# Moving the first activation buffer of a two-layer fp32 stack by 32 bytes in each SBUF partition

## Chip, core and metric

The kernel runs on one core of a Trainium2 chip. The metric is the device time of one execution in microseconds. The three runs shown for the kernel before lie between 2882.34 and 2883.41 us, with a median of 2883.28 us.

## What is computed

Two transformer-like layers on one sequence of 256 tokens with 2048 channels, all in fp32. The first layer has an input projection into a state-space mixer and an RWKV mixer, an output projection, cross attention to 256 memory tokens, and a feed-forward block of width 8192. The second has an input projection, windowed attention beside an S5 state-space branch, gated branch projections, and a gated feed-forward block of width 5632. Cut to its dense products:

```
u = rms_norm(x) @ w_in;  x = x + concat(ssd(u), rwkv(u)) @ w_out
x = x + cross_attention(rms_norm(x), rms_norm(mem), wq, wk, wv, wo)
x = x + square(relu(rms_norm(x) @ ffn_w1)) @ ffn_w2;  x = rms_norm(x)
proj = rms_norm(x) @ w_in_2;  attn, y = window_attention(proj), s5(proj)
x = x + (sig(ga)*(attn @ w_branch_attn) + sig(gs)*(glu(y) @ w_branch_ssm)) @ w_out_2
h = rms_norm(x);  x = x + (h@up_val * gelu(conv(h@up_gate))) @ w_down;  out = rms_norm(x)
```

## The kernel before

**Layout.** Channels lie on the 128 partitions, tokens along the free dimension. `x` is [128, 16, 256]. An operand of a dense product is kept as two parts whose sum is the fp32 value, a high part and a low part, both of type fp32r. An activation buffer holds both parts of each tile of 128 channels side by side: `[P, KT, 2, T]`, so one part of one tile is 256 values, 1024 bytes, in each partition.

**The stream of weights.** All dense products are phases of one pipeline (class `Stream`). A phase is a number of units (256 output columns of the weight), a unit is `nc` chunks (512 rows by 256 columns, 512 KB). For each chunk SP loads it into one of four ring slots (`raw`, line 320), ScalarE copies it to `hi` (`act_chunk`, line 379), VectorE writes `lo = raw - hi` (`split_low`, line 473), and TensorE multiplies it (`unit`). A chunk is 24 matmuls: two output halves by four channel tiles by a trio of part products. The trio is, with the stationary operand first and the moving operand second,

```
eng.matmul(out, self.hi[:, slot, cols], a[:, 0, :], start=opens, stop=False)
eng.matmul(out, self.hi[:, slot, cols], a[:, 1, :], start=False, stop=False)
ins = eng.matmul(out, self.lo[:, slot, cols], a[:, 0, :], start=False, stop=closes)
```

(lines 670, 671, 672). One phase, `wv` (kind "tok"), has the roles the other way round (lines 665 to 667): the activations `a[:, 0 or 1, toks]` are stationary and the 256 weight columns of `hi`, `hi`, `lo` are moving. After a unit VectorE reads its sums out of PSUM (`evacuate`), and ScalarE, VectorE or GpSimd write the next activations.

**Which activation buffer each phase reads.** There are 928 chunks. The first activation buffer `a0` is the moving operand of 568: `w_in` (14 + 6 + 4 units of 4), the two halves of `w_out` (16 each), `wk` (32), four quarters of `ffn1` (32 each), `w_in_2` (7 + 6 + 10 units of 4), `glu` (2 + 2), `br_ssm` (8), `up_gate` and `up_val` (22 units of 4 each). It is the stationary operand of the 32 chunks of `wv`. The other 328 read `a1` (`wq`, `wo`, four quarters of `ffn2`), `a2` (`w_out_2`, `down`) or `ah` (`br_attn`). Matmuls outside the pipeline are fp32 and belong to the mixers, the attentions and the norms.

**Places in a partition.** Tensors are laid on a stack one behind the other, and `room` tensors push the next one to a chosen address modulo `LINE` = 512 bytes. With the sizes in the code the places are these, in bytes modulo 512, before the change:

| tensor | place | tensor | place |
|---|---|---|---|
| x | 128 | a0 | 160 |
| consts, prm, rstd, root, sq, eps | 160 | sq2, gains | 192 |
| raw (all rings) | 160 | hi (all rings) | 224 |
| lo (all rings) | 352 | a1, a2, ah | 160 |
| ua, ub, u, kx, qx, vx, s_tab | 160 | s_xr | 192 |
| tb | 224 | th | 288 |

All rows of `a0`, `hi` and `lo` that one matmul reads begin at the place of their tensor, because 256 columns are 1024 bytes and half a unit is 512.

Of the kernel before, what the change touches and what calls it, by code (L numbers as in the profile page):

```python
# [25 lines left out]
P = 128  # L26
T = 256
D = 2048
KT = D // P
# [3 lines left out]
BASE = 128 + SCRATCH  # L33
LINE = 512
ACT_AT = 160
PART_AT = ACT_AT + 64
CK = 4
RING = 4
# [55 lines left out]
class Params:  # L94


    def __init__(self):
        self.at, self.n = {}, 0
# [6 lines left out]
PARAMS = Params()  # L105
# [85 lines left out]
class Stream:  # L191


    def __init__(self, nc, stack, dram):
        self.nc, self.dram = nc, dram

        def sb(name, shape, dt=F32):
            return stack.enter_context(nc.sbuf_tensor(name, shape, dt))

        def sem(name):  # L200
            return stack.enter_context(nc.semaphore(name))

        self.x = sb("x", [P, KT, T])
        at = BASE + KT * T * 4
        room = sb("a0_room", [P, (ACT_AT - at) % LINE // 4])
        self.a0 = sb("a0", [P, KT, 2, T], F32R)
        self.consts = sb("consts", [P, dram["consts"].shape[1]])
        self.prm = sb("prm", [P, PARAMS.n])
        self.rstd = sb("rstd", [P, T])
        self.root = sb("root", [P, T])  # L210
        self.sq = sb("sq", [P, 2, T])
        self.eps = sb("eps", [P, 8])
        self.sq2 = sb("sq2", [P, 2, T])
        self.gg = sb("gains", [P, KT])
        at += (ACT_AT - at) % LINE + KT * T * 8 + 4 * dram["consts"].shape[1] + -(-PARAMS.n // 8) * 32 + 6 * T * 4 + 32 + KT * 4
        room = sb("stage_room", [P, (ACT_AT - at) % LINE // 4])
        self.acc = stack.enter_context(nc.psum_tensor("acc", [P, 4, 512], F32))
        self.work = stack.enter_context(nc.psum_tensor("work", [P, 4, 512], F32))

        self.s_raw = [sem(f"raw_loaded{i}") for i in range(RING)]  # L220
        self.s_hi = sem("high_split")
        self.s_lo = sem("low_split")
        self.s_used = sem("chunk_multiplied")
        self.s_free = sem("banks_read")
        self.s_link = sem("vector_link")
        self.s_evac = sem("evacuated")
        self.s_fin = sem("finished")
        self.s_pool = sem("low_written")
        self.s_sum = sem("squares_summed")
        self.s_root = sem("root_ready")  # L230
        self.s_rstd = sem("rstd_ready")
        self.s_ehigh = sem("emitted_high")
        self.s_elow = sem("emitted_low")
        self.s_ghigh = sem("gained_high")
        self.s_glow = sem("gained_low")
        self.s_esq = sem("emitted_squares")
        self.s_first = sem("first_norm_steps")
        self.s_mean = sem("second_mean")
        self.s_root2 = sem("second_root")
        self.total = dict(c=0, u=0, links=0, evac=0, fin=0, pool=0, gain=0, norm=0, emits=0)  # L240
# [15 lines left out]
    def ring(self, stack, tag, parts=True, raw=None):  # L256
# [3 lines left out]
        def sb(name, shape, dt=F32):  # L260
            return stack.enter_context(nc.sbuf_tensor(name + tag, shape, dt))
        place = sb("raw", [P, RING, CK * UNIT])
        self.raw = place if raw is None else raw
        room = sb("ring_room", [P, (PART_AT - ACT_AT) // 4])
        self.hi = sb("hi", [P, RING, CK * UNIT], F32R)
# [2640 lines left out]
```

## Time and profile before

| | us |
|---|---|
| median of three runs | 2883.28 |
| lowest and highest run | 2882.34, 2883.41 |
| span of the profiled execution | 2882.9 |
| PE busy | 2802.8 (97%) |
| DVE busy | 1823.4 (63%) |
| ACT busy | 1245.7 (43%) |
| POOL busy | 396.0 (14%) |
| DMA, share of 16 engines | 54.9% |

Matmuls are pipelined: the duration of one runs from its start until its results are out, and the next starts before that. So the sum over the instructions of a line can be more than the time they fill, and the rate of the engine is read from starts, or from how many instructions fill a stretch. The profiled execution has no time of its own beside its span here; the span is 0.4 us under the median run.

### The profile page before, as it was taken

What the parts mean: (1) busy time and instruction counts of PE and PEld (TensorE: products, weight loads), DVE (VectorE), ACT (ScalarE), POOL (GpSimd) and SP (SyncE); (2) the same over time, 40 slices, a digit from 0 to 9 for tenths busy, and PEclk for the clock granted to TensorE, in tenths of its full rate; (3) what the DMA queues carried; (4) which work ended last, traced back from release to release, by engine and by line L of the source; (5) the groups of instructions that cost most, each with busy time, mean ns of one, the idle gap of its engine ahead of it and who ended that gap; (6) DMA issues with size and microseconds to landing.
All of it is one profiled execution on the core that took longest, in us unless ns stands there. A gap on an engine that the chain in (4) does not pass through costs nothing.

```text
span 2882.9 us, 61146 instructions
## 1 busy us (share of the span) xinstructions
PE 2802.8 (97%) x24650; PEld 2752.2 (95%) x24650; DVE 1823.4 (63%) x2175; ACT 1245.7 (43%) x1511; POOL 396.0 (14%) x549
## 2 busy tenths in 40 slices
PE   8999699999999999999999999999999999999998
PEld 8999687999989999999999999998999999999998
DVE  6678747775435655655555668697667655665664
ACT  5355223544334543444434545434454443443444
POOL 0000230110002139300461210000110000010011
PEclk9999899999999999999999999999999999999999
DMA  6654002566635566666667565554555665556564
GB/s 235 195 192 147 16 31 88 191 189 204 190 102 164 190 197 190 219 213 189 197 194 236 191 195 163 193 196 157 193 192 189 197 192 193 193 188 199 184 198 149
DMA packets 138418, 514.10 MB, mean 178 GB/s; under 512 B 15360, under 2 KB 15616, under 8 KB 136960
## 3 DMA queue, kind: packets, MB, share of 16 engines
q1 hardware_dynamic: 138240, 511.58, 54.9%
q8 instruction: 129, 2.11, 0.3%
q14 instruction: 49, 0.40, 0.0%
HBM read 503.12 MB, written 8.40 MB: 177 GB/s over the span
## 4 chain that ended last, share of the span: by engine, by line
PE 64%; DVE 4%; issue 1%; ACT 1%; DVEq 0%; ACTq 0%
PE acc L670 21%; PE acc L671 21%; PE acc L672 21%; DVE lo L473 1%; PE work L2170 0%; ACT hi L379 0%; DVE s_xr L2514 0%; PE acc L2203 0%; DVE tb L543 0%; DVE sq L2523 0%; DVE ua L2514 0%; DVE ub L2514 0%; DVE s_xr L2505 0%; DVE sq L2503 0%; DVE ta L2522 0%
## 5 line engine op out<-in xcount | busy, mean ns | idle before, releaser
L670 PE MATMUL acc<-a,hi 128*128 128x256 f32 x5504 | 1527.0, 277 | 16.3 <-DVE lo L473 14.5
L671 PE MATMUL acc<-a,hi 128*128 128x256 f32 x5504 | 1521.5, 276 | 0.0
L672 PE MATMUL acc<-a,lo 128*128 128x256 f32 x5504 | 1521.4, 276 | 0.0
L473 DVE TENSOR_TENSOR lo<-qx,hi 128x1024 fp32r<-128x1024 f32 x704 | 896.4, 1290 | 674.6 <-ACT hi L379 672.9
L670 PEld LDWEIGHTS acc<-a,hi 128*128 128x128 f32 x5504 | 1035.3, 188 | 20.5 <-issue 14.8
L671 PEld LDWEIGHTS acc<-a,hi 128*128 128x128 f32 x5504 | 1035.3, 188 | 0.8 <-issue 0.5
L672 PEld LDWEIGHTS acc<-a,lo 128*128 128x128 f32 x5504 | 1035.3, 188 | 0.0
L379 ACT ACTIVATE hi<-qx 128x1024 fp32r<-128x1024 f32 x704 | 733.9, 1057 | 646.4 <-PE acc L672 629.0
L620 POOL TENSOR_TENSOR a<-th,a 128x512 f32 (+1 forms) x64 | 84.9, 1327 | 1381.2 <-ACT a L424 1381.1
L473 DVE TENSOR_TENSOR lo_x<-next_raw,hi_x 128x1024 fp32r<-128x1024 f32 x128 | 162.2, 1281 | 115.0 <-ACT hi_x L379 115.0
L670 PE MATMUL acc<-a,hi_in 128*128 128x256 f32 x768 | 215.4, 280 | 9.8 <-DVE lo_in L473 9.8
L670 PE MATMUL acc<-a,hi_x 128*128 128x256 f32 x768 | 215.8, 281 | 5.8 <-DVE lo_x L473 5.8
L672 PE MATMUL acc<-a,lo_in 128*128 128x256 f32 x768 | 213.8, 278 | 0.0
L671 PE MATMUL acc<-a,hi_in 128*128 128x256 f32 x768 | 213.8, 278 | 0.0
L671 PE MATMUL acc<-a,hi_x 128*128 128x256 f32 x768 | 212.8, 277 | 0.0
L672 PE MATMUL acc<-a,lo_x 128*128 128x256 f32 x768 | 212.8, 277 | 0.0
L379 ACT ACTIVATE hi_x<-next_raw 128x1024 fp32r<-128x1024 f32 x128 | 133.9, 1058 | 144.2 <-PE acc L672 94.9
L473 DVE TENSOR_TENSOR lo_in<-raw_in,hi_in 128x1024 fp32r<-128x1024 f32 x96 | 115.4, 1222 | 68.2 <-ACT hi_in L379 68.1
L670 PEld LDWEIGHTS acc<-a,hi_in 128*128 128x128 f32 x768 | 146.1, 190 | 11.2 <-DVE lo_in L473 9.7
L670 PEld LDWEIGHTS acc<-a,hi_x 128*128 128x128 f32 x768 | 144.9, 189 | 8.5 <-issue 5.8
L671 PEld LDWEIGHTS acc<-a,hi_in 128*128 128x128 f32 x768 | 146.0, 190 | 0.3 <-issue 0.2
L672 PEld LDWEIGHTS acc<-a,lo_in 128*128 128x128 f32 x768 | 145.9, 190 | 0.0
(503 smaller groups left out, 2779.2 us busy)
## 6 DMA issues: line engine op xcount, KB each, us to landing
qx<-in_ffn SPq DMA_DIRECT2D x256, 512.0 KB, 4.2
raw_in<-in_w_in SPq DMA_DIRECT2D x96, 512.0 KB, 4.3
qx<-in_w_in SPq DMA_DIRECT2D x92, 512.0 KB, 3.7
qx<-in_up_gate SPq DMA_DIRECT2D x88, 512.0 KB, 4.2
qx<-in_up_val SPq DMA_DIRECT2D x88, 512.0 KB, 4.3
qx<-in_down SPq DMA_DIRECT2D x88, 512.0 KB, 4.2
next_raw<-in_wq SPq DMA_DIRECT2D x32, 512.0 KB, 4.3
next_raw<-in_wk SPq DMA_DIRECT2D x32, 512.0 KB, 4.3
```

Of the source, the lines that this page charges most:

```text
L379: eng.activation(self.hi[:, slot, :], self.raw[:, slot, :], ACT.Copy).then_inc(self.s_hi, 1)
L473: eng.tensor_tensor(self.lo[:, slot, :], self.raw[:, slot, :], self.hi[:, slot, :].bitcast(F32), ALU.subtract).then_inc(self.s_lo, 1)
L620: eng.tensor_tensor(out[:, :, 1, :], self.th[:, s], out[:, :, 0, :].bitcast(F32), ALU.subtract).then_inc(self.s_pool, 1)
L670: eng.matmul(out, self.hi[:, slot, cols], a[:, 0, :], start=opens, stop=False)
L671: eng.matmul(out, self.hi[:, slot, cols], a[:, 1, :], start=False, stop=False)
L672: ins = eng.matmul(out, self.lo[:, slot, cols], a[:, 0, :], start=False, stop=closes)
```

## The change

A constant `A0_AT` = 192 takes the place of `ACT_AT` = 160 where the room ahead of `a0` is sized. `a0` and the eight tensors behind it, up to `gains`, lie 32 bytes further on; `stage_room` shrinks from 416 to 384 bytes, so that `u` and everything behind it stays at its address. `x` stays. No instruction is added, removed or moved on any engine: the programs are the same but for addresses.

```
+A0_AT = 192
...
-        room = sb("a0_room", [P, (ACT_AT - at) % LINE // 4])
+        room = sb("a0_room", [P, (A0_AT - at) % LINE // 4])
         self.a0 = sb("a0", [P, KT, 2, T], F32R)
...
-        at += (ACT_AT - at) % LINE + KT * T * 8 + 4 * dram["consts"].shape[1] + -(-PARAMS.n // 8) * 32 + 6 * T * 4 + 32 + KT * 4
+        at += (A0_AT - at) % LINE + KT * T * 8 + 4 * dram["consts"].shape[1] + -(-PARAMS.n // 8) * 32 + 6 * T * 4 + 32 + KT * 4
         room = sb("stage_room", [P, (ACT_AT - at) % LINE // 4])
```

| modulo 512 | a0 | hi - a0 | lo - a0 | a1, a2, ah |
|---|---|---|---|---|
| before | 160 | 64 | 192 | 160 |
| after | 192 | 32 | 160 | 160 |

## Rows read from the trace of the kernel before

**Rows 1.** The page: span, and each engine's busy time.
```profile
span 2882.9 us, 61146 instructions
PE 2802.8 (97%) x24650; PEld 2752.2 (95%) x24650; DVE 1823.4 (63%) x2175; ACT 1245.7 (43%) x1511; POOL 396.0 (14%) x549
```

**Rows 2.** Groups by line, shapes apart, PE: count, busy us, mean ns, idle before.
```profile
L670 PE MATMUL acc<-a,hi 128*128 128x256 f32 x5504 | 1527.0, 277 | 16.3 <-DVE lo L473 14.5 <-issue 1.8
L670 PE MATMUL acc<-a,hi_x 128*128 128x256 f32 x768 | 215.8, 281 | 5.8 <-DVE lo_x L473 5.8
L670 PE MATMUL acc<-a,hi_in 128*128 128x256 f32 x768 | 215.4, 280 | 9.8 <-DVE lo_in L473 9.8
L670 PE MATMUL acc<-ah,hi 128*128 128x256 f32 x128 | 35.6, 278 | 0.9 <-DVE lo L473 0.9
```

**Rows 3.** Busy time in stretches, PE: from:to, length, busy (matmuls), clock, DMA share, GB/s.
```profile
747.24:837.68 90.44, 90.44 (x770) 1.00 0.50 152
1143.25:1230.29 87.04, 87.04 (x770) 1.00 0.66 218
1230.29:1317.33 87.04, 87.04 (x770) 1.00 0.66 204
2585.60:2672.64 87.04, 87.04 (x770) 1.00 0.63 197
```

**Rows 4.** Groups by line of the stretch 747.24:837.68, phase `wv`.
```profile
L665 PE MATMUL acc<-hi_x,a 128*128 128x256 f32 x256 | 72.2, 282 | 0.0
L666 PE MATMUL acc<-hi_x,a 128*128 128x256 f32 x256 | 71.9, 281 | 0.0
L667 PE MATMUL acc<-lo_x,a 128*128 128x256 f32 x255 | 71.1, 279 | 0.0
```

**Rows 5.** Groups by line of the stretch 1143.25:1230.29, `ffn1` reading a0.
```profile
L670 PE MATMUL acc<-a,hi 128*128 128x256 f32 x257 | 70.9, 276 | 0.0
L672 PE MATMUL acc<-a,lo 128*128 128x256 f32 x256 | 70.7, 276 | 0.0
L473 DVE TENSOR_TENSOR lo<-qx,hi 128x1024 fp32r<-128x1024 f32 x32 | 43.3, 1367 | 36.7 <-ACT hi L379 36.7
L379 ACT ACTIVATE hi<-qx 128x1024 fp32r<-128x1024 f32 x32 | 33.8, 1060 | 31.5 <-PE acc L672 28.0 <-DMA qx<-in_ffn 3.2
```

**Rows 6.** Stretches with all engines: busy (x) of PE, PEld, DVE, ACT, POOL.
```profile
450.00:572.00 122.00, 116.24 (x926) 104.88 (x925) 87.73 (x126) 56.32 (x78) 13.57 (x11) 0.98 0.47 156
1743.00:1976.00 233.00, 225.89 (x1841) 215.70 (x1840) 203.98 (x315) 103.30 (x181) 0.00 (x0) 1.00 0.54 179
```

**Rows 7.** Groups by line, fp32 matmuls of 256 columns, PE.
```profile
L1731 PE MATMUL acc<-kx,qx 128*128 128x256 f32 x32 | 7.1, 379 | 0.0
L2438 PE MATMUL acc<-s_xr,s_tab 128*128 128x256 f32 x32 | 9.5, 379 | 0.0
L2438 PE MATMUL acc<-ua,s_tab 128*128 128x256 f32 x16 | 4.8, 379 | 0.0
L772 PE MATMUL acc<-f,consts 128*16 128x256 f32 x16 | 3.6, 380 | 0.0
```

**Rows 8.** Line 1731: duration min/median/max, first and last start.
```profile
L1731 PE MATMUL acc<-kx,qx x32: 379/379/379, 846.0 to 852.7; 128*128 128x256 f32 x32
```

**Rows 9.** Starts on PE and PEld (weight loads) in two short stretches, us.
```profile
1199.83 0.28 PE L670 MATMUL acc<-a,hi 128*128 128x256 f32 x1
1199.83 0.19 PEld L671 LDWEIGHTS acc<-a,hi 128*128 128x128 f32 x1
1199.94 0.28 PE L671 MATMUL acc<-a,hi 128*128 128x256 f32 x1
1199.95 0.19 PEld L672 LDWEIGHTS acc<-a,lo 128*128 128x128 f32 x1
```

**Rows 10.** Groups by line, VectorE, tensors at different places.
```profile
L543 DVE TENSOR_TENSOR tb<-acc,rstd 128x512 f32<-128x512 f32 x93 | 63.6, 684 | 0.4 <-PE acc L672 0.3
L496 DVE TENSOR_TENSOR x<-acc,x 128x512 f32 (+1 forms) x88 | 60.1, 683 | 13.3 <-PE acc L672 13.3
```

## The prediction

> **What bounds the kernel now.** I read the page first: PE is busy 97% of a span of 2882.9 us, DVE 63%, ACT 43% [rows 1]. So the end is set by the matmuls, and the change can only matter through what it does to their rate, or through another engine becoming so slow that it takes over. Next the groups by line, with shapes apart, to see whether the matmuls wait: of the three large groups of line 670 the idle time ahead is 16.3, 5.8 and 9.8 us, nearly all for VectorE's low part, in more than 7,000 matmuls [rows 2]. PE simply runs one matmul after the other.
>
> The durations in these groups are not the rate, since matmuls overlap. For the rate I took stretches that hold exactly one phase, which is 32 chunks or 768 matmuls (the view counts 770, because it also counts those that reach in over the edges). A phase of `ffn1` that reads a0 takes 87.04 us, the phase behind it that reads a1 takes 87.04 us, and one of `down` that reads a2 takes 87.04 us [rows 3]. That is 87.04 / 768 = 113.3 ns for each matmul of 256 columns, whichever buffer is moving, all of them at place 160. The exactness is what to see here: no phase is held up by data. The starts say the same, 1199.83 and 1199.94, and the load of the next weights starts within 0.01 us of the matmul beside which it runs, 1199.83 and 1199.95 [rows 9]. So PE reads two operands from SBUF at the same time nearly all the time: the moving one of this matmul and the stationary one of the next.
>
> One phase is different. `wv`, with the same 768 matmuls of the same shape, takes 90.44 us at the same full clock [rows 3], 117.8 ns each: 3.40 us more for the phase, 4.43 ns more for each. Its matmuls last 282, 281 and 279 ns [rows 4] against 276 and 276 [rows 5], with no idle time ahead of them in either. Nothing was late there. What differs is which operand is read from where: in `wv` the weight parts at 224 and 352 are moving and a0 at 160 is being loaded, so that the loaded operand lies 64 or 192 bytes behind the moving one, modulo 512; in the other phases it lies 64 or 192 ahead. I take this as the one sign in the trace that the pair of addresses, or the roles, can cost PE time without any wait on a semaphore.
>
> **The change, part by part.** It adds, removes and moves no instruction. It changes addresses of three kinds.
>
> First, a0 as moving operand. This is 568 of 928 chunks, 568 x 24 = 13,632 of 22,272 matmuls (the total is three times the 7,168 of line 670 and the 256 of line 665, [rows 2, 4]). The load of `hi` now lies 32 bytes ahead of the moving operand in place of 64, that of `lo` 160 in place of 192. No row shows such a pair, so the price is bounded from both sides. The one end is nothing: 113.3 ns holds at two distances, +64 and +192, and +160 lies between them. The other end is that each pays what `wv` pays, 4.43 ns: 13,632 x 4.43 = 60.4 us. I choose between them like this. The distance +160 is bracketed by two distances at which nothing is paid, so I take zero for the third of the matmuls beside which `lo` is loaded. The distance +32 is not bracketed: on its other side, past zero, the trace has only -64 and -192, and both pay. So I take the price for the two thirds beside which `hi` is loaded, 9,088 matmuls. In `wv` the two matmuls that move `hi`, at distance -64, have 6 and 5 ns of the 14 that the trio is longer (6 + 5 + 3), so they pay 11/14 of 3 x 4.43 = 13.3 ns, 5.2 ns each. 9,088 x 5.2 = 47.3 us.
>
> Second, what of this lies under other waits. In the phases that run beside the mixers and the window attention PE is not quite full: 116.24 of 122.00 us and 225.89 of 233.00 us [rows 6]. The a0 chunks in and next to such stretches are 16 + 16 (`w_out`), 24 + 40 (`w_in_2`, its last 16 units) and 12 (`glu`, `br_ssm`), 108 of the 568; their share of the sum is 108 x 16 x 5.2 ns = 9.0 us. PE's idle time there is 5.8 + 7.1 = 12.9 us, so it could take up all of it or none. Part of that idle time is a wait for things that themselves come after matmuls. I take half, 4.5 us off.
>
> Everywhere else a slower PE is fully on the path. In the stretch of `ffn1` VectorE's low parts take 43.3 us and then wait 36.7 us for ScalarE, whose copies take 33.8 us and wait 28.0 us for PE to free a slot [rows 5]: both are ahead and will only wait longer. That is also the cover for the third kind.
>
> Third, the engines' own accesses to a0, `consts`, `prm`, `rstd` and the others, now 32 bytes further. VectorE's reads of 128x512 take 684 ns with `rstd` (160) and `tb` (224), 683 ns with `x` (128) [rows 10], so place does not show, and I cost it at nothing. If the a0 writes did become slower, the cover is the 36.7 us of waiting in 87.04; the first units of a phase that waits for its activations are the only places without it. The fp32 matmuls with `consts` have the same answer: those of 256 columns last 379 or 380 ns with the moving operand at 160 (`kx`, `ua`), 192 (`s_xr`) or 224 (`f2`, shown as `f`) [rows 7]. Bound on the other side: 2,378 of the 24,650 matmuls stand outside the pipeline [rows 1]; if all of them read a moved tensor, which they do not, 1 ns each would be 2.4 us.
>
> a0 as stationary operand is `wv` alone, 768 matmuls; its distances go from -64 and -192 to -32 and -160. It could lose its 3.4 us or pay as much again. I take zero, and 3.4 us either way goes into the range.
>
> **Sum.** 47.3 - 4.5 = 42.8 us on the profiled execution's 2882.9 us gives 2925.7 us; the median run is 0.4 us above that span, so I forecast 2926 us.
>
> [...]
>
> **The rivals.**
>
> *No change (2883 us, 2877.5 to 2889).* The cost in `wv` comes from the roles: a stationary operand that is a piece of an activation tile, and a moving one that is a weight. Or place counts only in steps coarser than 32 bytes, such as 64 or 128. For it: a0, a1, a2 and ah, at four different absolute addresses, give 113.3 ns to the last digit [rows 3]. Against it: nothing, but those four have the same place modulo 512, so they are no test. The sum is 2883.3 plus nothing.
>
> *All pay (2944 us, up to 2948).* +160 pays too: 60.4 us, and `wv` 3.4 us more at worst. Against it stand the free distances on both sides of +160.
>
> [...]
>
> [...]
>
> **How the numbers follow.** Faster 0.13. No change 0.27. Slower 0.60: 0.37 for the forecast (2905 to 2935), 0.15 for all pay (2935 to 2948), 0.08 for a small price (2889 to 2905), such as one matmul of the trio alone or 1 to 2 ns each. Within 0.2%, 5.8 us, is about what a measurement of this kernel can tell from no change. The predicted time is the likeliest case's, 2926. The range runs from the low end of no change, 2877, to all pay with `wv` on top, 2948: it leaves out the faster case and the little that lies above, 0.03 or so, which is under 2 in 10. Slower holds most of the chance; its own range is 2889 to 2948.
>
> **What the profile after would show.** A phase of `ffn1` or `up_val` that reads a0 should take 87.04 + 768 x 2/3 x 5.2 ns = 89.7 us, and the phases that read a1 and a2 still 87.04. Within a trio the matmuls beside which `hi` is loaded should start 5 ns later and the one beside which `lo` is loaded not; all three later means all pay. [...] If the a1 and a2 phases change as well, the cause isn't the pair of addresses. DVE and ACT groups should keep their mean times, with longer waits for PE.

## The result

The changed kernel takes 2944.32 us (median of four runs, 2940.81 to 2947.74) against 2883.35 us before: 61.0 us more, a ratio of 1.021 with a 95% interval of 1.0196 to 1.0225. The forecast was 2926 us, with a range up to 2948: the result lies inside the range, above the band of 2905 to 2935 that I had given to the forecast itself and in the band of the rival "all pay".

The page of the changed kernel, its span and busy times, which answer to [rows 1]:

```profile
span 2939.0 us, 61146 instructions
PE 2863.7 (97%) x24650; PEld 2813.4 (96%) x24650; DVE 1824.2 (62%) x2175; ACT 1246.2 (42%) x1511; POOL 396.0 (13%) x549
```

PE is 60.9 us longer busy with the same 24,650 matmuls. DVE, ACT and POOL do the same work in the same time to within 0.8 us. So all of it is in the rate of the matmuls. (The span grew by 56.1 us only, since PE's idle time shrank by 4.8.)

The same phases as in [rows 3], PE alone: from:to, length, busy (matmuls), clock, DMA share, GB/s. In this order `wv`, `ffn1` on a0, `ffn2` on a1, `down` on a2:

```profile
761.67:852.13 90.46, 90.46 (x770) 1.00 0.49 151
1161.25:1252.13 90.88, 90.88 (x770) 1.00 0.66 211
1252.13:1339.18 87.05, 87.05 (x770) 1.00 0.64 203
2635.89:2722.94 87.05, 87.05 (x770) 1.00 0.64 196
```

The phase on a0 went from 87.04 to 90.88 us: 3.84 us for 768 matmuls, 118.3 ns each in place of 113.3, 5.0 ns more. The phases on a1 and a2 kept their 87.0 us, `wv` its 90.4. Line numbers in this kernel are one higher. In groups by line of the same `ffn1` stretch the trio stands like this, to be read against [rows 5]:

```profile
L672 PE MATMUL acc<-a,hi 128*128 128x256 f32 x257 | 72.1, 281 | 0.0
L671 PE MATMUL acc<-a,hi 128*128 128x256 f32 x257 | 72.1, 281 | 0.0
L673 PE MATMUL acc<-a,lo 128*128 128x256 f32 x256 | 71.9, 281 | 0.0
L474 DVE TENSOR_TENSOR lo<-qx,hi 128x1024 fp32r<-128x1024 f32 x33 | 43.4, 1328 | 40.4 <-ACT hi L380 40.3
L380 ACT ACTIVATE hi<-qx 128x1024 fp32r<-128x1024 f32 x32 | 33.8, 1058 | 34.3 <-PE acc L673 31.6 <-DMA qx<-in_ffn 2.7
```

All three are longer, 281 against 276 ns, not two of three. From start to start it is 118.0 ns behind line 671, 119.0 behind 672 and 118.0 behind 673, where the load of `lo` runs beside line 672. VectorE and ScalarE only wait longer, 40.4 and 34.3 us where it was 36.7 and 31.5.

The timeline of PE where `ffn1` on a0 begins (start, duration):

```profile
1161.38 0.28 PE L671 MATMUL acc<-a,hi 128*128 128x256 f32 x1
1161.50 0.28 PE L672 MATMUL acc<-a,hi 128*128 128x256 f32 x1
1161.62 0.29 PE L673 MATMUL acc<-a,lo 128*128 128x256 f32 x1
1161.74 0.28 PE L671 MATMUL acc<-a,hi 128*128 128x256 f32 x1
1161.86 0.28 PE L672 MATMUL acc<-a,hi 128*128 128x256 f32 x1
```

The starts are 0.12 apart where they were 0.11. In whole ns they are no longer alike: the steps repeat every twelve matmuls as 114, 119, 117, 123, 115, 116, 120, 124, 116, 115, 118, 123, on average 118.3.

Where the time came from, by the first matmul of each stage in the two traces:

| stage | later by, us | 5.0 ns times its a0 matmuls |
|---|---|---|
| w_in, up to the RWKV scan | 8.0 | 11.5 |
| both halves of w_out | 2.6 | 3.8 |
| wq, wk | 3.8 | 3.8 |
| wv, cross attention | -0.2 | 0 |
| wo, four times ffn1 and ffn2 | 15.4 | 15.4 |
| w_in_2, first 52 chunks to the state space | 6.1 | 6.2 |
| w_in_2, last 40 chunks | 0.3 | 4.8 |
| glu, br_attn, br_ssm | 0.5 | 1.4 |
| w_out_2 | -1.6 | 0 |
| gate, val, down, three times | 21.2 | 21.1 |
| sum (13,632 matmuls) | 56.1 | 68.2 |

In `w_out_2`, which reads a2, the trace before has a spell at the lower clock (granted 0.98 over the stage, 88.78 us) and the one after has none (1.00, 87.17 us). The same holds for one chunk of `w_in`, before and after:

```profile
262.67:267.14 4.47, 4.47 (x25) 0.62 0.80 257
271.83:274.77 2.94, 2.94 (x25) 1.00 0.88 304
```

Some 1.6 us of the 3.5 us that are missing in the first row of the table are this spell and no wait. The profiled execution after is the fastest of the four, 3.5 us under their median, which is the larger part of why 56.1 us stand under the 61.0 of the medians.

### The profile page after: what moved, and what is told of

Same layout as the page of the kernel before. It is cut to its first block, busy times and chain, and to the rows that moved or that the text cites. A ratio compares the mean times of both kernels' runs of the same rounds, so it can differ in the third digit from the quotient of the medians.

```text
span 2939.0 us, 61146 instructions
## 1 busy us (share of the span) xinstructions
PE 2863.7 (97%) x24650; PEld 2813.4 (96%) x24650; DVE 1824.2 (62%) x2175; ACT 1246.2 (42%) x1511; POOL 396.0 (13%) x549
## 4 chain that ended last, share of the span: by engine, by line
PE 65%; DVE 3%; issue 1%; ACT 0%; DVEq 0%; ACTq 0%
PE acc L673 21%; PE acc L671 21%; PE acc L672 21%; DVE lo L474 1%; PE work L2171 0%; ACT hi L380 0%; DVE s_xr L2515 0%; PE acc L2204 0%; PE work L2427 0%; DVE ua L2515 0%; DVE tb L544 0%; DVE x L1916 0%; DVE sq L2504 0%; PE work L2191 0%; DVE sq L2524 0%
## 5 line engine op out<-in xcount | busy, mean ns | idle before, releaser
L671 PEld LDWEIGHTS acc<-a,hi_x 128*128 128x128 f32 x768 | 145.4, 189 | 8.2 <-issue 5.6
L672 PEld LDWEIGHTS acc<-a,hi_x 128*128 128x128 f32 x768 | 145.3, 189 | 0.6 <-issue 0.5
```

## The experiments

Two theories at the start. A: what counts is the distance from the operand that is moving to the operand that is being loaded. B: what counts is the place of the moving operand, a multiple of 64 bytes (192) or not (160).

**e1: weight parts 32 bytes nearer, all activations at 160.**

```
-PART_AT = ACT_AT + 64
+PART_AT = ACT_AT + 32
...
-        room = sb("end_room", [P, (LINE - 128) // 4])
+        room = sb("end_room", [P, (LINE - 96) // 4])
```

> All activation buffers at 160 as before, the weight parts 32 bytes nearer: hi at 192, lo at 320, so that every phase has the distances that the change gave to a0 (32 and 160). Theory A, the distance from the moving operand to the loaded one sets the price: all 21,504 matmuls with activations moving pay 5.0 ns, about +107 us, 2990 us. Theory B, the place of the moving operand on a 64-byte border sets it: none of the phases pays, 2883 us, each phase of 32 chunks 87.0 us; only wv, whose moving operands then lie on such a border, may change, by about 4 us.

2985.51 us (two runs), ratio 1.0351, interval 1.0305 to 1.0397. Now the phases on a0 and on a1 both pay (PE in stretches):

```profile
1173.88:1264.76 90.88, 90.88 (x770) 1.00 0.65 209
1264.76:1355.64 90.88, 90.88 (x770) 1.00 0.63 196
```

The same 90.88 us as in the changed kernel, with no activation buffer moved. Theory B falls. The two runs lie 9.9 us apart, so the total is known less well than the phases.

**e2: everything 32 bytes on.**

```
-ACT_AT = 160
+ACT_AT = 192
```

> Everything is moved by 32 bytes together: activation buffers at 192, hi at 256, lo at 384, distances 64 and 192 as before. Theory A (distance): 2883 us, phases of 32 chunks at 87.0 us. Theory B (moving operand on a 64-byte border): every phase pays 5.0 ns per matmul, 21,504 x 5.0 = 107 us, about 2990 us, phases at 90.8 us.

2883.79 us (eight runs), ratio 0.9997, interval 0.9985 to 1.0008.

```profile
1143.15:1230.19 87.04, 87.04 (x770) 1.00 0.67 218
1230.19:1317.23 87.04, 87.04 (x770) 1.00 0.67 205
```

With a0 at 192 and the weight parts moved with it, the cost is gone to the last digit. Theory A holds so far: what counts is where the two operands lie to each other.

**e3: a0 at 224.** The changed kernel with `A0_AT = 224`, distances 0 and 128.

> a0 alone at 224, another 32 bytes on: distance to hi 0 and to lo 128, off the 64-byte border again. Theory A: at least the price of distance 32, so 2944 us or more. Theory B: back to 113.3 ns per matmul, 2883 us.

2950.57 us (two runs), ratio 1.0229, interval 1.02 to 1.0259. The a0 phase takes 91.47 us, 119.1 ns each, although 224 is no more a multiple of 64 bytes than the 160 at which it took 87.04 us.

**e6 and e7: one distance wrong at a time.** Both start from e2. In e6 `low_room` has 96 bytes in place of 128 (and `end_room` 32 more), which gives distances 64 and 160. In e7 `PART_AT` is `ACT_AT + 32` and `low_room` 160 bytes: 32 and 192.

> Activations at 192, hi at 256, lo at 352: distances 64 and 160. My forecast had zero for a lo at distance 160: then every phase stays at 87.0 us per 32 chunks, 2883 us. If lo at 160 pays by itself (a third of the price measured, about 1.7 ns per matmul on average), 88.3 us per phase and about 2920 us. If the trio pays whole as soon as one distance is off, 90.8 us per phase and about 2985 us.

> Activations at 192, hi at 224, lo at 384: distances 32 and 192. My forecast had 5.2 ns for two of three matmuls: 89.7 us per phase of 32 chunks, about 2955 us. If the trio pays whole as soon as one distance is off: 90.8 us per phase and about 2985 us. If only lo at 160 was what cost in the changed kernel: 87.0 us and 2883 us.

2966.39 and 2976.64 us (one run each). PE in the a0 phase, e6 first, then e7:

```profile
1167.11:1257.56 90.45, 90.45 (x770) 1.00 0.67 210
```
```profile
1175.68:1266.13 90.45, 90.45 (x770) 1.00 0.68 210
```

Either error alone costs 3.41 us of the 3.84 that both cost together, so the two prices do not add up. Within the trio the two kernels differ. In e6 the steps behind lines 670, 671 and 672 are 114.0, 123.3 and 116.0 ns, and the long one is the one beside which `lo`, the part that stands wrong, is loaded (starts on PE and on PEld):

```profile
1199.86 0.28 PE L671 MATMUL acc<-a,hi 128*128 128x256 f32 x1
1199.87 0.19 PEld L672 LDWEIGHTS acc<-a,lo 128*128 128x128 f32 x1
1199.99 0.28 PE L672 MATMUL acc<-a,lo 128*128 128x256 f32 x1
1200.10 0.28 PE L670 MATMUL acc<-a,hi 128*128 128x256 f32 x1
```

In e7 they are 118.7, 118.3 and 116.3 ns: the matmul beside which `lo` is loaded pays 5.0 ns although `lo` stands right. So a load that stands wrong costs at its own place and can cost beside a right one too; a sum of prices, one for each load, gives neither kernel. (The two totals differ by 10 us with equal long phases. 8.6 of them are there before `ffn1` begins, where e7 has 14 us more at the lower clock (mean granted clock over the whole span 0.989, in e6 0.992) and stretches of chunks at 120.0 ns.)

**e4: a table of single pairs.** 16 moving by 16 stationary places, each pair 36 matmuls long, one behind the other.

> A kernel that leaves out the whole computation but for a copy of x, and runs 36 back-to-back fp32r matmuls of 256 columns for each of 16 moving places by 16 stationary places (steps of 32 bytes modulo 512), with nothing on the other engines. Moving 160 with stationary 224 or 352 should take 113.3 ns each, moving 192 with 224 or 352 118.3 ns, moving 224 with stationary 160 118 ns. Theory A: the time is a function of the difference of the two places. Theory B: 113.3 for moving places at 32 modulo 64, 118 for multiples of 64, whatever the stationary place; then moving 224 or 352 with stationary 160 would be 113.3 here and the price of wv would be of its roles.

Of the 256 pairs 249 took 116.7 to 120.1 ns on average (the very first, at 162.8, left out), and only six 113.3 to 113.5. All six are at distance 64 modulo 256, but the other pairs at that distance took 117.8, moving 160 with stationary 224 among them. So the distance alone, for one pair repeated, does not decide. This is a miss: moving 160 with stationary 224 was expected at 113.3. The slow values repeat every 256 bytes of distance: 120.0 ns at 0 and 256, 118.3 at 32 and 288, 120.0 at 160 and 416.

**e5 and e11: tables of trios.** The trio of the kernel in place of a single pair. In e11 with the addresses of a whole chunk:

```
for i in range(8):
    t, q = divmod(i, 4)
    cols = slice(q * T + t * P, q * T + (t + 1) * P)
    eng.matmul(out, hi[:, h // 4:][:, cols], act[:, q, 0, :], ...)
    eng.matmul(out, hi[:, h // 4:][:, cols], act[:, q, 1, :], ...)
    eng.matmul(out, lo[:, l // 4:][:, cols], act[:, q, 0, :], ...)
```

> A kernel that leaves out the computation but for a copy of x. It runs the trio of the pipeline (hi, hi, lo as stationary, the two parts of an activation tile as moving) 20 times in a row for each of 8 by 8 distances of hi and of lo from the activations, 0 to 224 bytes in steps of 32, with the activations at 160 and at 192, then the same with the roles turned as in wv. PE waits between groups, so that each starts afresh. If the pair of distances (hi, lo) sets the time: (64, 192) gives 113.3 ns at both places and (32, 160) 118.3 ns at both. If the absolute place matters, the tables for 160 and 192 differ.

> A kernel that leaves out the computation but for a copy of x. It runs two chunks of 24 matmuls with the very addresses of the pipeline (four channel tiles, two output halves) for 16 by 16 distances of hi and lo over the whole 512 bytes; once after a wait, once right behind 12 matmuls at distances (64, 192); then turned chunks as in wv for 8 by 8 distances. If the fast state depends on the distances alone: the two tables agree, (64, 192) is at 113.3 ns and (448, 64), the place of a0 at 288, at 118.9. If it can be inherited: (448, 64) and others are at 113.3 behind fast matmuls and slow after a wait, or the other way round, and (32, 160) is slow in both.

In e5 the table with the activations at 160 and that at 192 agree to 0.1 ns in all but the first cell. From e11, after a wait, mean ns between starts over the last 24 matmuls (rows: distance of hi; columns: distance of lo):

```
          0    32    64    96   128   160   192   224
    0 120.0 118.3 117.8 119.1 119.1 117.8 118.0 117.8
   32 117.8 118.3 118.5 117.5 118.3 118.3 117.8 118.2
   64 117.8 120.2 113.3 117.8 118.2 117.8 113.3 117.3
   96 118.5 117.8 118.9 117.4 118.9 118.3 117.8 117.8
  128 118.3 118.3 117.8 120.0 118.8 117.8 116.7 120.0
  160 117.8 121.1 117.8 119.6 117.8 120.0 117.8 120.0
  192 117.8 117.8 113.3 117.8 115.5 117.8 117.8 117.8
  224 117.8 117.8 119.5 118.9 117.8 117.8 118.9 116.7
```

This table gives the kernels' numbers in the long phases: (64, 192) 113.3 as before; (32, 160) 118.3 as after and in e1; (0, 128) 119.1 as in e3; (64, 160) and (32, 192) 117.8 as in e6 and e7. The fast rate is the exception, three cells of 64. Turned as in `wv` (activations stationary, weight parts moving), with the addresses of a chunk, no cell of 64 is fast, the lowest is 116.7, and (64, 192) is at the 117.8 of `wv`.

Right behind 12 other matmuls, which run at (64, 192), the table is mostly the same, but (192, 192) is fast in it too. Over the whole 512 bytes, 256 cells in each table, there is an order in this: behind the 12 matmuls exactly the sixteen cells are fast in which both distances are 64, 192, 320 or 448, that is 64 modulo 128; after a wait ten of these sixteen are, and no other. So the pair of distances decides whether the fast rate can be had, and for some of these pairs the way in decides whether it is.

**e8: a0 at 288.** Distances 448 and 64, which modulo 256 are the fast cell (192, 64).

> The changed kernel with a0 at 288 in place of 192: moved by 128 bytes from its old place, not by 32. Its distances to hi and lo, counted modulo 256, are 192 and 64, one of the three pairs that ran at 113.3 ns in the table of trios. If the table with its period of 256 bytes is the rule: 2883 us, all phases on a0 at 87.0 us per 32 chunks, and wv as before. If any departure of a0 from the place of the other buffers costs, as the change did: about 2940 us or more.

2941.53 us (four runs), ratio 1.0183, interval 1.0167 to 1.0199: a miss for the table taken alone. It is the number that the other theory of this experiment gave, that any departure of a0 from the place of the other buffers costs; but in e1, e6 and e7 all buffers share a place and pay, and a part of the a0 chunks here runs at the fast rate. PE in the stretches of `ffn1` on a0, `ffn2` on a1, and the first 28 chunks of `w_in_2` on a0:

```profile
1166.68:1257.99 91.31, 91.31 (x770) 1.00 0.65 211
1257.99:1345.04 87.05, 87.05 (x770) 1.00 0.65 202
1701.74:1780.20 78.46, 78.46 (x682) 1.00 0.63 191
```

One pair of places, and two rates: `ffn1` runs at 118.9 ns throughout. In `w_in_2` the first four chunks run at 118.9, then come eight fp32 matmuls of a norm, some 215 ns apart, and the other 24 chunks run at 113.3. In the second half of `w_out` it goes the other way, nine chunks and then five:

```profile
545.62:570.11 24.49, 24.49 (x218) 1.00 0.70 254
573.00:587.27 14.27, 14.27 (x123) 1.00 0.56 185
```

That is 113.4 and 118.9 ns. Between them stands a chunk that begins with one step of 156 ns. So the fast rate, once reached, can also be lost.

**e9: `wv` placed by the table.** The kernel before, with hi in `wv` alone 128 bytes further on.

```
+    def high(self, ph, slot):
+        at = TURNED_AT if ph.kind == "tok" else 0
+        return self.hi[:, slot, at:at + CK * UNIT]
```

> The kernel before, with hi in the phase wv alone written and read 128 bytes further on (slots of the ring of that stage are 256 bytes longer, so that they stay apart). With turned roles hi and lo then both lie at distance 192 from a0, the one pair that ran at 113.3 ns in the table of turned trios. If the table is the rule: wv takes 87.0 us in place of 90.4, everything else as before, 2880 us. If the price of wv is of its roles and not of its places: 90.4 us and 2883 us.

2884.52 us (eleven runs), ratio 0.9998, interval 0.9989 to 1.0007, and `wv`, the second row here, is as it was (the first is `wk`):

```profile
661.92:748.96 87.04, 87.04 (x770) 1.00 0.66 204
748.96:839.41 90.45, 90.45 (x770) 1.00 0.49 152
```

The pair (192, 192) had been fast in e5, where each trio used the same addresses, and is at 117.8 in e11, where they step as in a chunk; `wv` is at 117.8 here. e5 was too simple a copy of that phase. No version faster than the kernel before came out of this. The first row shows one thing more: the longer slots put every second slot of hi at distance 320 in place of 64, and `wk` keeps its 87.04 us, so 256 bytes more or less do not matter there.

**e10: other lengths and fp32.**

> A kernel that leaves out the computation but for a copy of x. It runs groups of 60 like matmuls, each group afresh, for 128 to 512 moving columns and eight distances from the moving to the loaded operand in steps of 32 bytes, then finer distances around 64 at 256 columns, then the same eight distances in fp32. If the stream of the moving operand is what is held up, the price of a bad distance stays or grows at 384 and 512 columns; if the load of the weights is, it is there at 128 to 256 columns and gone at 384 and 512, where the matmul is much longer than a load. In fp32 no distance should matter (216 ns).

Mean ns between starts, lowest and highest of eight distances from 0 to 224: 128 columns 111.7 to 111.7; 192 columns 111.7 to 111.7; 256 columns 116.7 to 120.0; 288 columns 131.7 to 133.4; 320 columns 146.6 to 146.7; 384 columns 173.3 to 176.7; 512 columns 226.7 to 234.3; fp32, 256 columns, 215.8 to 215.9. At 128 and 192 columns the step is the same and the distance costs nothing; something other than the columns sets the pace there, and this run does not show what. Between the distances lie 3.3 ns at 256 columns, 1.7 at 288, 0.1 at 320, 3.4 at 384 and 7.6 at 512: no steady growth, but a cost also where the matmul is twice as long as in the kernel. So it does not look as if the load alone were held up. In fp32, where every matmul takes 216 ns, nothing shows. At 256 columns the distances 52 and 88 were fast, 113.3, though none of the eight was, and 48 and 56 not: the steps of 32 bytes hide finer structure.

**e12: the same places, alone and in company.** Ten chunks in a row for five pairs of distances, alone, with semaphores at each chunk ("marked"), beside ScalarE, beside VectorE, beside all; twice.

> A kernel that leaves out the computation but for a copy of x. It runs ten chunks with the addresses of the pipeline in a row for five pairs of distances, among them (64, 192) of the kernel before and (448, 64) of a0 at 288, which was fast for 48 matmuls alone but slow in most phases of the kernel. Each pair is run alone, with a semaphore counted and tested at every chunk, beside ScalarE copies, beside VectorE subtractions, and beside all three; all of it twice. If something beside the matmuls throws a pair out of the fast state and only some pairs come back: (64, 192) is at 113.3 ns in every mode, (448, 64) falls to 118.9 in the mode that does it. If (448, 64) stays at 113.3 in all modes, the reason for its loss in the kernel is none of these. (32, 160) is at 118.3 everywhere.

Alone, 240 matmuls each, in this order (64, 192), (448, 64), (192, 64), (32, 160) (PE: length, busy):

```profile
13.20:41.88 28.68, 28.56 (x238) 1.00 0.00 1
42.21:70.74 28.53, 28.47 (x240) 1.00 0.00 1
71.07:98.30 27.23, 27.17 (x240) 1.00 0.00 1
...
126.17:154.70 28.53, 28.47 (x240) 1.00 0.00 1
```

The first row begins with 13 steps of some 213 ns, hence its length; all ten groups of (64, 192) step at 113.3 ns from at most the eighth trio on. With semaphores at each chunk, (64, 192), (448, 64) and (32, 160):

```profile
155.02:182.28 27.26, 27.20 (x240) 1.00 0.01 1
182.69:209.87 27.18, 27.05 (x239) 1.00 0.01 1
...
266.54:294.91 28.37, 28.25 (x239) 1.00 0.00 1
```

The pair of e8 has both rates: 28.53 us (118.9 ns) alone and 27.18 us (113.3 ns) where each chunk counts a semaphore. It is not the counting that does it: the first semaphore is counted by the 24th matmul, and the steps are at 113 ns from the second on. What differs before it is the very first step, 194 ns against 227. Beside ScalarE's copies and beside VectorE's subtractions, (64, 192) and (448, 64) each (PE, PEld, DVE, ACT, POOL):

```profile
295.32:322.53 27.21, 27.09 (x239) 27.12 (x239) 0.00 (x0) 25.48 (x24) 0.00 (x0) 1.00 0.00 1
322.85:351.39 28.54, 28.48 (x240) 28.42 (x240) 0.00 (x0) 25.45 (x24) 0.00 (x0) 1.00 0.01 1
435.67:462.92 27.25, 27.19 (x239) 27.13 (x239) 24.51 (x20) 0.00 (x0) 0.00 (x0) 1.00 0.00 1
463.25:491.78 28.53, 28.47 (x240) 28.41 (x240) 24.50 (x20) 0.00 (x0) 0.00 (x0) 1.00 0.00 1
```

24 ScalarE or 20 VectorE instructions beside the matmuls change neither rate. Over all ten groups of each: (64, 192) ten times fast; (192, 64) ten times; (64, 64) nine times, once 117.8; (448, 64) four times fast, six times 118.9; (32, 160) never fast, at 118.3 four times and at 118.9 six times. No group of e12 that had reached the fast cycle left it; in the kernel of e8 one did.

## Why the prediction came out as it did

**That the matmuls are the path, and that nothing else would show: right.** PE's busy time grew by 60.9 us, DVE, ACT and POOL kept theirs. In the long phases every ns was on the path, 15.4 of 15.4 and 21.2 of 21.1 us.

**That the pair of addresses is what counts, read from the one odd phase `wv`: right.** e1 and e2 show it, one by making the loss without moving an activation buffer, the other by taking it away with a0 at 192. The rival of no change falls: two addresses alone took the step from 113.3 to 118.3 ns. Nor did anything become faster, to which the forecast gave 0.13: the a0 phase, 87.04 us before, takes 90.88 us in the changed kernel and in e1, 87.04 in e2 and 91.47 in e3. The lowest mean step of 256 columns in any phase or table here is 113.3 ns.

**How I got there from `wv`: in part luck.** The forecast took the 117.8 ns of `wv` as the price of its distances, -64 and -192. The table of turned chunks in e11 has no fast cell at all, and e9 moved hi in `wv` and gained nothing. So `wv` may be slow by its roles wherever its operands lie, and its distances say little about a0 at +32. That `wv` itself would not change was right: 90.46 us after, 90.44 before.

**The step that failed: "The distance +160 is bracketed by two distances at which nothing is paid, so I take zero for the third of the matmuls".** The forecast gave each load a price of its own, by its own distance, and put the one of `lo` at nothing. e6 has hi at 64 and only lo at 160, and pays 3.41 us a phase, where that step says zero, 10.0 ns of a trio's 13.3 at the very matmul beside which lo is loaded. In the changed kernel this matmul pays 5.7 ns and the other two 4.7. e7 has only hi wrong and pays the same 3.41 us, spread over all three matmuls. There is no price that belongs to one load, and no interpolation between distances. What ties the time of one matmul to the whole trio, no run shows. That 113.3 ns "holds at two distances, +64 and +192" was in truth one observation, of one trio, and not two points of a curve.

**The size.** The rival "all pay" took 4.43 ns from `wv` for each of the 13,632 matmuls, 60.4 us and 2944 us. It met the median, by two errors that cancel: the price was 5.0 ns (68.2 us in all), and by the medians 7.2 us of it did not reach the end. The forecast had 5.2 ns for 9,088 matmuls, 47.3 us. Its 5.2 ns, split by durations, was near the 5.0 that the starts give for the same two matmuls in `wv`; what was wrong was the number of matmuls that pay. It missed 18 of the 61 us, and its range held the result only because it reached up to the rival.

**What lies under other waits: right in kind, too small.** I took 4.5 us off. The table of stages has 3.5 us missing in `w_in`, of which some 1.6 are the spell at the lower clock, 1.2 in `w_out`, 4.5 in the last 40 chunks of `w_in_2` and 0.9 behind it, so some 8.5 us taken up by waits. The 1.6 us in `w_out_2` are again a spell that only the trace before has. In the last 40 chunks of `w_in_2` nearly all of it went under: PE's idle time in the stretch of [rows 6] fell from 7.1 us to 3.7.

**What stays open.** Why (64, 192) came to 113.3 ns in every group and table, why all fast cells of e11 have both distances at 64 modulo 128, and what in SBUF or in PE has such a period, no run shows. The pair (32, 160) has two slow cycles, 118.3 and 118.9 ns, in e12 and also in the profiled execution of the changed kernel. There the phases of `ffn1`, `up_gate` and `up_val` are at 118.3 wherever PE does not wait, but 22 chunks near the start of `w_in_2` are at 118.9 (62.78 us):

```profile
1711.12:1773.90 62.78, 62.78 (x531) 1.00 0.59 183
```

The spread of the four runs after, 6.9 us against 2.8 before, could come from phases that fall now into the one and now into the other (13,632 x 0.56 ns = 7.6 us at most). But it is no firm sign: the nine runs of the kernel before beside e1 lie 5.0 us apart, and the mean granted clock of the four runs goes from 0.989 in the slowest to 0.991 in the fastest.

## What to carry to other kernels

Where fp32r matmuls of 256 columns run back to back with a weight load beside each, treat the places of the two operands relative to each other as a tuning parameter: here they were worth 4% of such a phase (90.88 us against 87.04) and 2% of the kernel (2944.32 against 2883.35). The kernel before has the loaded parts 64 and 192 bytes ahead of the moving one, and its long phases stayed at 87.04 us when both were moved together (e2). Look at the step between starts, in whole phases, since the busy share (97% before and after) hides it. When one phase of equal shape is slower without a wait, addresses are one thing to try, though for `wv` itself no better place was found (90.45 us in e9). A price read off one pattern of addresses holds for that pattern as a whole, so try a new placement in the kernel itself, with its real strides and entries, before believing a table.

## What the runs showed of the hardware that was not expected

- One pair of addresses can have two lasting rates, 113.3 and 118.9 ns per matmul, on the same program text. In e12 each group of (448, 64) whose first step took 192 to 194 ns ran at 113.3, and each with 227 or 228 ns at 118.9; in e8 the rate went from 118.9 to 113.3 behind eight fp32 matmuls and from 113.4 to 118.9 behind a step of 156 ns.
- The fast cycle (113.3 ns) is rare: 3 of 64 pairs of distances, after a wait (e11), and none of 64 with the roles turned, where the lowest is 116.7. Behind 12 matmuls at (64, 192) it was had at 16 of 256 pairs, those with both distances 64 modulo 128. (64, 192), the kernel's own, was reached in all ten groups of e12 and in both tables.
- The cost goes with the places of PE's own two operands and not with other engines. 24 copies on ScalarE or 20 subtractions on VectorE beside 240 matmuls changed nothing (at (64, 192) 27.21 and 27.25 us, against 27.23 for (192, 64) alone; at (448, 64) 28.54 and 28.53, alone 28.53).
- It depends on the length of the moving operand, not steadily (none at 192 columns, 3.3 ns between the distances at 256, 0.1 at 320, 7.6 at 512), and is absent in fp32 at 215.8 ns (e10).
